# A loop over expert blocks on TensorE: block 0 moved into the loop, which starts two turns sooner

## The reference

```python
h = rmsnorm(x, norm_mix[i]);  proj = h @ w_in[i]
mix = concatenate([retention(...), diff_attention(...)])
x = x + mix @ w_out[i]
h = rmsnorm(x, norm_ffn[i])
x = x + hierarchical_moe(h, ...)      # top-1 of 4 groups, then top-2 of its 4 experts
gate = sigmoid(rmsnorm(x, norm_ple[i]) @ w_ple_gate[i])
x = x + gate * (p[i] @ w_ple_proj[i]);  return rmsnorm(x, norm_final)
```

## Time and profile before

| | us |
|---|---|
| median of three runs | 646.67 |
| profiled execution | 648.02 |
| its span, first to last instruction | 646.2 |
| TensorE busy | 589.2 (91%) |
| VectorE, ScalarE, GpSimd busy | 212.9, 199.3, 51.5 |
| mean granted clock of TensorE | 0.959 of full speed |
| moved by DMA | 151.52 MB, mean 234 GB/s |

### The profile page before, as it was taken

One profiled execution on the slowest core, in us unless ns is written; L12 is line 12 of the kernel. 1 busy time (PEld: TensorE's weight loads), 2 busy tenths in 40 slices (PEclk: granted clock), 3 DMA queues, 4 the chain that ended last, 5 costly groups with the idle time before them and its releaser, 6 DMA issues.

```text
span 646.2 us, 9470 instructions
## 1 busy us (share of the span) xinstructions
PE 589.2 (91%) x3456; PEld 382.4 (59%) x3457; DVE 212.9 (33%) x475; ACT 199.3 (31%) x434; POOL 51.5 (8%) x91
## 2 busy tenths in 40 slices
PE   6999999999999999999678999999999987926994
PEld 6998877878989999974222333333333332304883
DVE  3621264565444343277000111101111010064653
ACT  5532354555543543342100001001010010062774
POOL 0000000000000000000201121121221211110000
PEclk9899999999999999989797999999999999986998
DMA  9743123203210249836696499999999999934001
GB/s 317 199 172 131 65 66 131 65 8 125 66 66 1 66 166 420 354 139 256 245 422 246 183 421 420 421 421 421 421 422 421 422 418 421 410 115 182 33 33 65
DMA packets 47216, 151.52 MB, mean 234 GB/s; under 512 B 7880, under 2 KB 27216, under 8 KB 34640
## 3 DMA queue, kind: packets, MB, share of 16 engines
q1 hardware_dynamic: 43504, 139.77, 55.2%
q0 software_dynamic: 3392, 11.02, 4.4%
q10 hardware_dynamic: 288, 0.29, 0.2%
HBM read 141.63 MB, written 9.45 MB: 234 GB/s over the span
## 4 chain that ended last, share of the span: by engine, by line
PE 79%; DMA 7%; DVE 6%; issue 3%; SPq 2%; ACT 2%; DVEq 0%; POOLq 0%; POOL 0%; ACTq 0%
PE bank L1598 19%; PE bank L1320 13%; PE bank L1321 12%; PE bank L1322 12%; PE bank L1624 10%; DMA ring_dn<-in_w_down 5%; PE bank L1402 2%; SPq L585 2%; PE bank L1584 2%; PE bank L1375 2%; DVE ple_lo L1253 2%; DMA gmix<-in_norm_mix 1%; PE bank L1527 1%; PE bank L1610 1%; PE bank L1416 1%
## 5 line engine op out<-in xcount | busy, mean ns | idle before, releaser
L1598 PE MATMUL bank<-ring_gu,rowsT 128*64 128x512 f32 (+1 forms) x800 | 147.0, 608 | 6.6 <-issue 3.0
L1598 PEld LDWEIGHTS bank<-ring_gu,rowsT 128*64 128x64 f32 (+1 forms) x800 | 44.2, 129 | 94.5 <-issue 90.3
L1624 PE MATMUL bank<-ring_dn,hidT 128*64 128x512 f32 (+1 forms) x400 | 75.8, 606 | 7.0 <-DMA ring_dn<-in_w_down 3.7
L880 ACT ACTIVATE silu_g<-bank 128x256 f32<-128x256 f32 x20 | 7.7, 383 | 224.0 <-PE bank L1598 224.0
L1069 DVE TENSOR_TENSOR w_lo<-w_raw,w_hi 128x2048 fp32r<-128x2048 f32 x18 | 41.3, 2292 | 76.9 <-ACT w_hi L745 69.6
L1219 DVE TENSOR_TENSOR hid<-silu_g,bank 128x256 f32<-128x256 f32 x20 | 8.4, 421 | 153.4 <-ACT silu_g L880 153.4
L1320 PE MATMUL bank<-w_hi,hT_hi 128*128 128x256 f32 x192 | 56.1, 292 | 0.9 <-issue 0.9
L1321 PE MATMUL bank<-w_lo,hT_hi 128*128 128x256 f32 x192 | 54.9, 286 | 0.0
L1322 PE MATMUL bank<-w_hi,hT_lo 128*128 128x256 f32 x192 | 54.9, 286 | 0.0
L1320 PE MATMUL bank<-hT_hi,w_hi 128*128 128x512 f32 x128 | 50.8, 397 | 0.0
L1321 PE MATMUL bank<-hT_lo,w_hi 128*128 128x512 f32 x128 | 49.9, 390 | 0.0
(11 more groups left out here) (214 smaller groups left out, 902.0 us busy)
## 6 DMA issues: line engine op xcount, KB each, us to landing
ring_gu<-in_w_gate SPq DMA_DIRECT2D x32, 1024.0 KB
ring_gu<-in_w_up SPq DMA_DIRECT2D x32, 1024.0 KB
ring_dn<-in_w_down SPq DMA_DIRECT2D x16, 2048.0 KB, 21.3
w_raw<-in_w_in SPq DMA_DIRECT2D x14, 1024.0 KB, 5.0
w_raw<-in_w_out SPq DMA_DIRECT2D x4, 1024.0 KB, 4.9
ple_gate_raw<-in_w_ple_gate SPq DMA_DIRECT2D x1, 4096.0 KB, 28.9
yg<-y_rows SPq DMA_DIRECT2D x8, 512.0 KB, 7.4
xr<-in_x SPq DMA_DIRECT2D x4, 512.0 KB, 9.1
```

What stands on the lines that cost most here:

```text
L1598: last = T.matmul(b_gu[q * BLK + t:q * BLK + t + n, :], rowsT[:, k % 4, k // 4, t:t + n], ring_gu[s][:, :, k, q * UC:(q + 1) * UC], start= ...
L1624: last = T.matmul(b_dn[q * BLK + t:q * BLK + t + n, :], hidT[:, kf % 2, kf // 2, t:t + n], ring_dn[s][:, kf, q * (D // 2):(q + 1) * (D // 2)],
```

## The change

TensorE's loop covers block 0 too. It runs over 26 turns, t from 0; turn t does gate_up of block t-1, rows_transpose of block t, down of block t-2, and hidden_transpose of block t-1 at its end, under `If(t > 0)`. `blk_code` gets two entries in front, with the pair number 6 (`NO_PAIR`), which no variant matches. So in turn 0 neither gate_up nor down does a product: the sequencer loads the code, and each test sends it past a variant's code to the next test. In turn 1 gate_up is block 0's, and down again finds no variant. The halving of the list becomes a linear chain: test for variant 0, else test for variant 1, and so on, with a test for the sixth too. The wait for `ple_ready` moves into the variants whose first slot is 0. Semaphore thresholds shift by one, and VectorE gives `y_ready` 2 and `hidT_ready` 1 at the start. VectorE has one more memset, ahead of L1030.

```diff
-        blk_code = tiny("blk_code", [1, MAX_BLOCKS], I32)
+        blk_code = tiny("blk_code", [1, 2 + MAX_BLOCKS], I32)
...
-                pool.wait_ge(y_ready, b + 2)
+                pool.wait_ge(y_ready, b + 3)
...
+                V.memset(blk_code[:, 0:2], LOADS_0 + LOADS_1 + NO_PAIR)
...
-                V.scalar_tensor_tensor(blk_code[:], q_of[:, :, 1], float(LOADS_1), code[1][:],
+                V.scalar_tensor_tensor(blk_code[:, 2:], q_of[:, :, 1], float(LOADS_1), code[1][:],
...
-            dve.sem_inc(y_ready, 1)
+            dve.sem_inc(y_ready, 2)
+            dve.sem_inc(hidT_ready, 1)
...
                 def one_of(pairs):
-                    if len(pairs) == 1:
-                        products(pairs[0], loads)
-                        return
-                    first, rest = pairs[:len(pairs) // 2], pairs[len(pairs) // 2:]
-                    with pe.If(pair < 2 * rest[0][0] + (rest[0][0] != rest[0][1])):
-                        one_of(first)
-                    with pe.Else():
-                        one_of(rest)
+                    slots = pairs[0]
+                    with pe.If(pair < 2 * slots[0] + (slots[0] != slots[1]) + 1):
+                        products(slots, loads)
+                    if pairs[1:]:
+                        with pe.Else():
+                            one_of(pairs[1:])
...
                 def products(slots, loads):
-                    pe.wait_ge(xT_ready, b + 1)
+                    pe.wait_ge(xT_ready, t)
+                    if slots[0] == 0:
+
+                        pe.wait_ge(ple_ready, 2 * NT)
...
-            rows_transpose(0, 1)
-
-            pe.wait_ge(ple_ready, 2 * NT)
-            gate_up(0, pairs=[(0, 0), (0, 1)])
-            rows_transpose(1, 1)
-
-            def step(b, k, turn):
-                hidden_transpose(b - 1)
-                gate_up(b)
-                with pe.If(turn % ROW_BUFS < 1):
-                    rows_transpose(0, turn // ROW_BUFS + 2)
-                with pe.Else():
-                    rows_transpose(1, turn // ROW_BUFS + 2)
-                down(b - 1)
-
-            over_blocks(pe, total, step, group=1)
-            hidden_transpose(total - 1)
-            down(total - 1, pairs=[(0, 0), (2, 0)])
+            with pe.Fori(0, MAX_BLOCKS + 1) as t:
+                with pe.If(t < total + 1):
+                    gate_up(t)
+                    with pe.If(t % ROW_BUFS < 1):
+                        rows_transpose(0, t // ROW_BUFS + 1)
+                    with pe.Else():
+                        rows_transpose(1, t // ROW_BUFS + 1)
+                    down(t)
+                    with pe.If(t > 0):
+                        hidden_transpose(t)
+            down(total + 1, pairs=[(0, 0), (2, 0)])
```

More of the change, by code:

```diff
@@ L55 @@
 LOADS_1 = 64
+NO_PAIR = 6
 GPE = SEQ // GRP
@@ L1552, in _, with in_slots @@
             ANY = [(0, 0), (0, 1), (1, 1), (1, 2), (2, 2), (2, 0)]
[L1554 to L1560, removed]
-                def one_of(pairs):
-                    if len(pairs) == 1:
-                        products(pairs[0], loads)
-                        return
-                    first, rest = pairs[:len(pairs) // 2], pairs[len(pairs) // 2:]
-                    with pe.If(pair < 2 * rest[0][0] + (rest[0][0] != rest[0][1])):
-                        one_of(first)
-                    with pe.Else():
-                        one_of(rest)
+            def in_slots(n, products, pairs=ANY):
+                code = pe.value_load(blk_code[0:1, bass.ds(n, 1)], min_val=LOADS_0 + LOADS_1, max_val=8 * LOADS_1 - 1)
+                pair, loads = code % LOADS_0, [code // LOADS_0 % (LOADS_1 // LOADS_0), code // LOADS_1]
+                def one_of(pairs):
+                    slots = pairs[0]
[4 more added lines that the diff above has]
+                            one_of(pairs[1:])
                 one_of(pairs)
@@ L1585, in rows_transpose, with gate_up @@
                 last.then_inc(xT_done, 1)
-            def gate_up(b, pairs=ANY):
+            def gate_up(t):
                 def products(slots, loads):
-                    pe.wait_ge(xT_ready, b + 1)
+                    pe.wait_ge(xT_ready, t)
+                    if slots[0] == 0:
+                        pe.wait_ge(ple_ready, 2 * NT)
                     for k in range(KD):
@@ L1596, in products @@
                                 pe.wait_ge(s_gu[slots[1]][k // (KD // 2)], 32 * loads[1])
-                        for q, t, n, s in column_tiles(slots):
-                            last = T.matmul(b_gu[q * BLK + t:q * BLK + t + n, :], rowsT[:, k % 4, k // 4, t:t + n],
+                        for q, c, n, s in column_tiles(slots):
+                            last = T.matmul(b_gu[q * BLK + c:q * BLK + c + n, :], rowsT[:, k % 4, k // 4, c:c + n],
                                             ring_gu[s][:, :, k, q * UC:(q + 1) * UC],
@@ L1603, in products, with hidden_transpose @@
                     last.then_inc(gu_done, 1)
-                in_slots(b, products, pairs)
-            def hidden_transpose(b):
-                pe.wait_ge(hid_ready, b + 1)
+                in_slots(t + 1, products)
+            def hidden_transpose(t):
+                pe.wait_ge(hid_ready, t)
                 for j in range(2):
@@ L1611, in hidden_transpose, with down @@
                 last.then_inc(hT_done, 1)
-            def down(b, pairs=ANY):
+            def down(t, pairs=ANY):
                 def products(slots, loads):
-                    pe.wait_ge(hidT_ready, b + 1)
-                    pe.wait_ge(y_ready, b + 1)
+                    pe.wait_ge(hidT_ready, t)
+                    pe.wait_ge(y_ready, t)
                     pe.wait_ge(s_dn[slots[0]], 16 * loads[0])
@@ L1622, in products @@
                     for kf in range(D_EXPERT // P):
-                        for q, t, n, s in column_tiles(slots):
-                            last = T.matmul(b_dn[q * BLK + t:q * BLK + t + n, :], hidT[:, kf % 2, kf // 2, t:t + n],
+                        for q, c, n, s in column_tiles(slots):
+                            last = T.matmul(b_dn[q * BLK + c:q * BLK + c + n, :], hidT[:, kf % 2, kf // 2, c:c + n],
                                             ring_dn[s][:, kf, q * (D // 2):(q + 1) * (D // 2)],
@@ L1627, in products @@
                     last.then_inc(dn_done, 1)
-                in_slots(b, products, pairs)
-            rows_transpose(0, 1)
-            pe.wait_ge(ple_ready, 2 * NT)
-            gate_up(0, pairs=[(0, 0), (0, 1)])
-            rows_transpose(1, 1)
-            def step(b, k, turn):
-                hidden_transpose(b - 1)
-                gate_up(b)
-                with pe.If(turn % ROW_BUFS < 1):
-                    rows_transpose(0, turn // ROW_BUFS + 2)
-                with pe.Else():
-                    rows_transpose(1, turn // ROW_BUFS + 2)
-                down(b - 1)
-            over_blocks(pe, total, step, group=1)
-            hidden_transpose(total - 1)
-            down(total - 1, pairs=[(0, 0), (2, 0)])
+                in_slots(t, products, pairs)
+            with pe.Fori(0, MAX_BLOCKS + 1) as t:
[9 more added lines that the diff above has]
+            down(total + 1, pairs=[(0, 0), (2, 0)])
             def x2_transpose(i):
```

## The result

The changed kernel takes 651.2 us (median of 20 runs, 646.49 to 655.15), the kernel before 647.43 beside it (20 runs): ratio 1.0068 (it goes by all runs; the two medians alone would give 1.0058), interval 1.0039 to 1.0096, or 2.5 to 6.2 us more. That lies inside the forecast range and within 1%, as given the chance of 0.75; but the forecast was +1.1 us, and the interval starts above it.

What follows compares the result with a forecast made beforehand. TensorE was taken to bound the expert stage, the end moving with gate_up of block 3. Price 11.9 plus memset 0.1 less gain 10.9 made +1.1 us on 646.67, so 647.8 us; range 641 to 655.

Steps and rivals of the forecast that it cites:

- The end moves with gate_up of block 3: Expert stage: the kernel's end shifts one for one with the start of block 3's gate_up.
- The price of the walk: Turn 0, before block 0: three code fetches waited for in sequence start block 0 at 324.7, not 312.76; 11.9 us lost.
- The gain: Blocks 0 to 3: code already present, so fetch gaps and the slow clock behind them go; 10.9 us gained.
- block 0 to block 3 takes 12.14, plus 0.4, plus 2 x 11.70: Time from gate_up of block 0 to that of block 3: 35.9 us against 46.9.
- a half clock in block 1, which would add 3 us: Sign of a wrong forecast: block 1's products at half clock (7.09 becoming 10.06), adding 3 us.
- Longer chains: Each regular turn: up to six tests, not three, need 3.1 to 3.6 of 3.73 us, so no cost.
- The tail: Stage end: last transpose no longer stands behind the empty turns; 0 to 0.5 us comes back, counted as nothing.
- Cheap walk: Turn 0: fetches overlap or hide behind the wait for gathered rows, block 0 near 314, -9.6 us, 637; chance 0.08.
- Four blocks at full price: Turn 0: four fetches of 6.1 us each, block 0 at 336.0, net +12.4 us, 659; chance 0.10.
- Loop longer than the store: Loop code: first blocks gone when the last arrives, gaps stay, only delay is new, +12.0 us, 658.7; chance 0.04.
- Chain gaps: Every turn: longer test chains open a gap of 0.6 us in 19 turns, sum +6.1 us, 653; chance 0.05.

Runs made afterwards that it cites:

- the walk under routing: Changed kernel with turn 0 started after the third PLE product, routing and other PLE products inside it: 641.29 us, ratio 0.9896 to the kernel before.
- the second execution before: The kernel before the change, unedited, profiled once more: 649.84 us.
- the kernel with the transpose at the head: Changed kernel with the hidden transpose moved from a turn's end to the head of the next: 652.52 us, ratio 1.0065 to the kernel before.
- The halved list: Changed kernel with the variant list split in two at each test again, plus a test for the last variant: 651.8 us, ratio 1.0050 to the kernel before.
- the dummy products: Changed kernel with five extra products in turn 0, ahead of the second chain of tests: 649.49 us, ratio 1.0023 to the kernel before.

## Why the prediction held, and what was off

- **The end moves with gate_up of block 3**: held. From there to the end are 286.6 and 289.1 us before, 287.0 to 289.5 after (ledger), and 1.7 us of the spread is the last down at 3.67 or 5.37. These five profiles have block 3 at 358.9 to 364.0; with 351.1, in the walk under routing, some 2 us more passed behind it, so "one for one" isn't shown that far.
- **The price of the walk**, 11.9 us from three fetches of 3.2, 3.8 and 6.1: held, +11.8 (block 0 at 325.22, forecast 324.7). Its two assumptions were tested one at a time: one block of code more costs 2.5 us, and with the DMA engines idle in its second half the walk is 2.2 us shorter. My split of 3.0 idle against 6.1 loaded makes that 2.7 to 3.1 us. The parts bear it out: where products seem to have waited for a packet, they came 2.2 to 3.1 us after its start, in ten profiles (before: 333.75 to 336.08; here: 314.1 to the transposes of block 0's rows at 316.54), so with 2.3 the third block, begun at 320.2, can be used at 322.5, as forecast. From there to block 0 are 2.7 us, forecast 2.2. The fourth packet starts at 323.3, only 1.9 us ahead of block 0 (1.2 to 2.0 in the eight profiles with a walk ahead of block 0). That is too short for one that was waited for, so three waited fetches is the likely count; no run removes the fourth.
- **The gain**: the fetch gaps went, as forecast, and with them the slow down of block 0 and the slow gate_up of block 2. The tests behind the transpose cost 0.3 us more ahead of block 1 (1.88 against 1.58; forecast 0.4).
- **The term that was mis-sized** is in the same step, "block 0 to block 3 takes 12.14, plus 0.4, plus 2 x 11.70". It carried block 0's gate_up over at its old 9.07 us and took block 1 at 7.09. Behind a walk in which TensorE does 1.13 us of products in 14, block 0 took 10.03, 10.12 and 9.50, and block 1 took 8.44, 8.48 and 7.09. That is 2.3, 2.4 and 0.4 us over the forecast's values, 1.7 on the mean; with 0.2 by which the second execution before was shorter (46.47 against 46.86, half of it in the mean) it is the whole difference of 10.9 and 9.0. The forecast named "a half clock in block 1, which would add 3 us" as what would make it wrong; it came at 1.4 us, in two executions of three.
- **In the runs** slow stretches show without a profile, but not where they lie. Of the 20 of the changed kernel, 8 had a mean granted clock of 0.950 or less and took 653.5 to 655.2 us, 7 had 0.957 and took 649.8 to 650.6. Of 52 runs of the kernel before none was under 0.951. The profiled execution with a slow block 1 alone had 0.951, the one with a slow last down as well 0.950, and the kernel with the transpose at the head has 0.949 in 5 of 12 runs too. So the clocks fit the slow block 1 and don't single it out.
- **Longer chains**: nothing, as forecast. The halved list gives the same time, and a regular turn is still 11.70 us (363.46 to 375.16). The margin is as thin as the forecast said: in its three profiles a few products start 0.10 to 0.16 us late, behind a pause of kind issue.
- **The tail**: counted nothing. From the end of down of block 18 to the last down are 2.70 us (569.59 to 572.29), before 2.56 (565.25 to 567.81): nothing came back.
- **The rivals.** *Cheap walk*: not here; moved under routing, the walk became nearly that (5.6 us to block 0). *Four blocks at full price*: no; block 0 comes 17.0 to 17.6 us after the gather, and a block of code added to the loop gives +2.5 us. *Loop longer than the store*: no, since no fetch falls between 345 and 560 us. The Trainium skill, in "Runtime: NRT & Kernel Launch", section "Instruction fetch mechanics", calls the store two lines wide in one paragraph and gives TensorE 128 KB in another; four packets of 16 KB each that serve all 20 blocks speak against two lines. How much TensorE holds in all no run here shows. *Chain gaps*: no.

What stays open: the ledger's mean is +3.3 us and the medians' +3.8, which the interval of 2.5 to 6.2 doesn't tell apart; 0.4 of the 3.3 is a later start of the gather, and the starts of one kernel differ by up to 1.7 us between executions. That the slow block 1 costs the median 1.4 us in 40% or more of the executions is argued from three profiles and the clocks, not shown by an experiment: the dummy products cured block 0 and left block 1 slow. Not tried: dummy products behind the gap of block 1, and the walk under routing with them.

## What to carry to other kernels

Code that is walked in advance costs what its fetches cost, one after another, so the walk belongs under a wait that is there anyway: the same walk cost 11.8 us where TensorE was on the path, and beside routing nothing that stands out of the spread, with 6.6 us of gain in the median against the kernel before. When a stall of TensorE is moved, move its slow clock with it in the sum: add what the first products behind it pay, and take that from rows behind a pause of the same length, not from the old place. And before dropping written-out code ahead of a loop, ask what is fetched while it runs.

## What was not expected of the hardware

- The same loop, entered without a walk, met seven fetches and 12.5 us of gaps, while the kernel before met 6.9 us (1.58, 2.41, 1.48, 1.46) with block 0 written out: first use of code behind forward jumps was dearer than the five regular fetches made me think.
- The clock fell a second time in block 1, behind a pause of 3.4 us (335.25 to 338.61), after it had come back in block 0. Over all profiles with a walk, the two gate_ups together take 15.6 to 18.6 us, where 14.0 would be full speed, and the split between them changes. The Trainium skill, "TensorE: Matmul & The Clock Gate", Part 1, says that the number of slow products at a start varies from run to run of one kernel; the three executions of the changed kernel agree.
- Fetches take longer beside bulk loads: 4.61 us in place of 6.92 for the second half of the walk, with 2.5 MB of loads moved out of its way (2048 KB of w_down, 512 KB of the final gain).
